# A matrix-state recurrence on one core: masked and turned chunk products interleaved under the state chain, and a query scaling without its own exponential

## What is computed

```python
def step(S, inp):
    r_t, d_t, k_t, v_t, kk_t, a_t = inp
    sk = jnp.einsum('bhvk,bhk->bhv', S, kk_t)
    S = (S * d_t[:, :, None, :] - sk[..., None] * (kk_t * a_t)[:, :, None, :]
         + v_t[..., None] * k_t[:, :, None, :])
    return S, jnp.einsum('bhvk,bhk->bhv', S, r_t)
```

## Time and profile before

| | us |
|---|---|
| median of 3 runs | 3968.01 (3967.4 to 3968.58) |
| the profiled execution, its own time | 3959.53 |
| its span in the profile | 3957.7 |
| PE busy in the span | 3685.2 (93%) |
| DVE busy | 2278.2 (58%) |
| ACT busy | 825.3 (21%) |
| mean granted clock of PE | 0.978 of full speed |

### The profile page before, as it was taken

The page is one execution under the profiler, slowest core; times in us unless marked ns, Lnnn a source line. Parts: engine busy times, 40 slices in busy tenths (PEclk is TensorE's granted clock), DMA queues, the critical chain, the costliest instruction groups (busy, mean ns, idle before and its releaser), DMA issues. The chain is left out here.

```text
span 3957.7 us, 73111 instructions
## 1 busy us (share of the span) xinstructions
PE 3685.2 (93%) x31536; PEld 2846.8 (72%) x31536; DVE 2278.2 (58%) x3422; ACT 825.3 (21%) x1844; POOL 741.0 (19%) x504
## 2 busy tenths in 40 slices
PE   7999788888899999999998999999967999999997
PEld 4888566666666888877776777777644788887886
DVE  8441677776446666672646455556555666666253
ACT  6110444333221110010112222222223101101000
POOL 1221000000022222213432101001002222221343
PEclk9999899999899999999999999999988999999999
DMA  2222111100121111112322111111482111112232
GB/s 81 84 75 85 61 32 37 34 30 27 65 88 45 36 45 45 45 61 82 114 78 72 49 43 51 40 47 40 138 310 109 47 45 45 45 35 80 82 110 75
DMA packets 119160, 268.30 MB, mean 68 GB/s; under 512 B 38073, under 2 KB 59961, under 8 KB 116409
## 3 DMA queue, kind: packets, MB, share of 16 engines
q1 hardware_dynamic: 118840, 263.63, 19.2%
HBM read 214.64 MB, written 48.95 MB: 67 GB/s over the span
## 5 line engine op out<-in xcount | busy, mean ns | idle before, releaser
L403 PE MATMUL ps<-sb_h,sb_w 128*128 128x272 f32 x1672 | 408.1, 392 | 1.4 <-ACT sb_tmp L563 1.4
L403 PEld LDWEIGHTS ps<-sb_h,sb_w 128*128 128x128 f32 x1672 | 317.5, 190 | 67.6 <-issue 2.3
L403 PE MATMUL ps<-sb_x,sb_w 128*128 128x272 f32 x1216 | 291.1, 392 | 0.0
L403 PEld LDWEIGHTS ps<-sb_x,sb_w 128*128 128x128 f32 x1216 | 231.0, 190 | 47.6
L460 PE MATMUL ps<-sb_big,sb_w 128*128 128x272 f32 x1056 | 251.6, 397 | 2.5 <-issue 1.3
L460 PEld LDWEIGHTS ps<-sb_big,sb_w 128*128 128x128 f32 x1056 | 202.5, 192 | 46.5 <-issue 4.3
L766 DVE SCALAR_TENSOR_TENSOR sb_big<-sb_tmp,sb_big 128x1024 f32<-128x1024 f32 (+1 forms) x176 | 203.4, 1156 | 13.2
L1454 PE MATMUL ps<-sb_x,sb_w 128*128 128x272 f32 x768 | 183.8, 392 | 0.0
L373 PE MATMUL ps<-sb_h,sb_w 128*128 128x384 f32 (+1 forms) x576 | 177.1, 469 | 3.9 <-DVE sb_tmp L741 2.1
L2682 PE MATMUL ps<-sb_h,sb_w 128*128 128x384 f32 (+1 forms) x528 | 171.8, 468 | 0.0
L1454 PEld LDWEIGHTS ps<-sb_x,sb_w 128*128 128x128 f32 x768 | 145.9, 190 | 30.1
(11 more groups left out here) (415 smaller groups left out, 7015.9 us busy)
## 6 DMA issues: line engine op xcount, KB each, us to landing
sb_w<-wup SPq DMA_DIRECT2D x88, 512.0 KB, 4.5
sb_w<-wdown SPq DMA_DIRECT2D x48, 704.0 KB, 4.2
sb_w<-wqkv SPq DMA_DIRECT2D x33, 512.0 KB, 3.7
sb_w<-wrkv SPq DMA_DIRECT2D x24, 512.0 KB, 5.6
sb_tmp<-wdown SPq DMA_DIRECT2D x16, 704.0 KB, 4.2
sb_x<-kT SPq DMA_DIRECT2D x10, 1024.0 KB, 12.1
rkv_scratch<-sb_big SPq DMA_DIRECT2D x18, 544.0 KB, 6.5
sb_big<-vc SPq DMA_DIRECT2D x9, 1024.0 KB, 11.7
```

The source lines that it names most:

```text
L403: mm = pe.matmul(m.ps[:, 2 * HOME[f][p] + e, 0:PIECE], w, rhs[:, k, e * PIECE:(e + 1) * PIECE], start=(k == 0 and p not in ("P2", "P3")), ...
```

## The change

`PIPE` and the three orders now alternate: two masked units, the two turned units that had come late, and one gate unit, three times (`at` `bt`, `kq` `kt`, `rb` `vt`), and then `rk` and `bv`. `CHAIN` follows that order. DVE does `normal_key`, the addition and the decay of the samples' state one each between the two steps that go with the turned units. In `decays` the subtraction is gone, in `powers` its exponential; `scale_q` multiplies Q by `EP` of the token before, in each chunk from its second token on (in the sample chunk in each group of 8), with a drain ahead of it.

```diff
--- before.py
+++ after.py
@@ -1475,11 +1475,13 @@
     SC = NCH - 1
     LAST = PAIRS - 1
 
+    FRONT = (("at", "bt"), ("kq", "kt"), ("rb", "vt"), ("rk", "bv"))
     PIPE = [(0, "sa", 0), (0, "sa", 1), (0, "sa", 2), (0, "kn")]
     for i in range(PAIRS):
         prev, ahead = i > 0, i < LAST
         gate = [[(i + 1, "sa", g)] if ahead else [] for g in range(3)]
-        PIPE += [(i, "at"), (i, "kq"), (i, "rb")] + gate[0] + [(i, "rk")] + ([] if i else [(0, "bonus")]) + gate[1] + [(i, "bt")] + gate[2] + [(i, "kt"), (i, "vt"), (i, "bv")]
+        for n, (masked_st, turned_st) in enumerate(FRONT):
+            PIPE += [(i, masked_st)] + ([(0, "bonus")] if n == 3 and not i else []) + [(i, turned_st)] + (gate[n] if n < 3 else [])
         PIPE += ([(i - 1, "ys")] if prev else []) + [(i, "t0")]
         for l in range(1, 6):
             PIPE += [(i, f"t{l}"), (i, f"z{l - 1}")]
@@ -1502,9 +1504,7 @@
         who = "a" if u[1] in BY_ACT else "d"
         counts[who] += 1
         TAKEN[u] = (who, counts[who])
-    CHAIN = {}
-    for n, st in enumerate(("at", "kq", "rb", "rk", "bt", "kt", "vt", "bv")):
-        CHAIN[st, 0], CHAIN[st, 1] = 2 * n + 1, 2 * n + 2
+    CHAIN = {u: n + 1 for n, u in enumerate((st, half) for st in ("at", "bt", "kq", "kt", "rb", "vt", "rk", "bv") for half in range(2))}
     STEPS = PC
     APART = {"at", "kq", "rb", "rk", "bv", "t1", "x1", "t2", "x2", "G", "H", "yl"}
     WHOLE = {"t0", "qt"}
@@ -1724,8 +1724,7 @@
 
             def powers(j):
                 act.wait_ge(prep_d, prepared(j, "diff"))
-                act.activation(EP, LS, ACT.Exp, scale=-DEC)
-                act.activation(SG, SG, ACT.Exp, scale=-DEC).then_inc(acts, 1)
+                act.activation(EP, LS, ACT.Exp, scale=-DEC).then_inc(acts, 1)
 
             def inverse_powers(j):
                 act.activation(LS, LS, ACT.Exp, scale=DEC)
@@ -1769,14 +1768,10 @@
             for i in range(PAIRS):
                 ahead = i + 1 if i < LAST else None
                 act.wait_ge(prep_d, prepared(i, "ready"))
-                if ahead:
-                    gates(ahead, 0)
-                    gates(ahead, 1)
-                turned_out(i, "bt", BTc)
-                if ahead:
-                    gates(ahead, 2)
-                turned_out(i, "kt", KTc)
-                turned_out(i, "vt", VTc)
+                for n, (st, dst) in enumerate((("bt", BTc), ("kt", KTc), ("vt", VTc))):
+                    turned_out(i, st, dst)
+                    if ahead:
+                        gates(ahead, n)
                 if ahead:
                     squares(ahead)
                 out(i, "bv", BVc)
@@ -1820,9 +1815,7 @@
 
             def decays(j):
                 wait_taken(dve, j, "sa", 2)
-                dve.tensor_tensor_scan(LS, reset, SG, 0.0, ALU.mult, ALU.add)
-                dve.drain()
-                dve.tensor_tensor(SG, LS, SG, ALU.subtract).then_inc(prep_d, 1)
+                dve.tensor_tensor_scan(LS, reset, SG, 0.0, ALU.mult, ALU.add).then_inc(prep_d, 1)
 
             def keys(j):
                 dve.tensor_scalar(EI, A, -1.0, col(j, PKA), ALU.add, ALU.mult)
@@ -1862,7 +1855,10 @@
 
             def scale_q(j):
                 dve.wait_ge(acts, ACTS[j, "powers"])
-                dve.tensor_tensor(Qt[j % 2], Qt[j % 2], SG, ALU.mult)
+                dve.drain()
+                for lo, hi, n in ((0, SEQ, C), (SEQ, T, NS)):
+                    q, before = (t[:, lo:hi].rearrange("p (c s) -> p c s", s=n) for t in (Qt[j % 2], EP))
+                    dve.tensor_tensor(q[:, :, 1:n], q[:, :, 1:n], before[:, :, 0:n - 1], ALU.mult)
 
             def scale_b(j):
                 dve.wait_ge(acts, ACTS[j, "inverses"])
@@ -1881,22 +1877,19 @@
                 dve.scalar_tensor_tensor(out=dst, in0=m.ps[:, 7, 0:HD], scalar=pend[i % 2][:, c:c + 1],
                                          in1=Nc[:, c, :], op0=ALU.mult, op1=ALU.add).then_inc(std, 1)
 
-            def steps(i, *sts):
...
-            def mask(i, st, which, dst):
-                for half in range(2):
-                    if i and CHAIN[st, half] < PC:
-                        step(i - 1, CHAIN[st, half])
-                    wait_full(dve, i, st, half)
-                    ins = dve.tensor_tensor(octet(dst, half), octet_ps(i, st, half), bc2(ms[:, which, :]), ALU.mult)
-                    for r, src in samples_out(i, st) if half else []:
-                        ins = dve.tensor_tensor(dst[r, SC, :], src, ms[r, which + 2, :], ALU.mult)
-                    ins.then_inc(outd, 1)
+            def chained(i, st, half):
+
+                if i and CHAIN[st, half] < PC:
+                    step(i - 1, CHAIN[st, half])
+
+            def mask(i, st, which, dst, half):
+
+                chained(i, st, half)
+                wait_full(dve, i, st, half)
+                ins = dve.tensor_tensor(octet(dst, half), octet_ps(i, st, half), bc2(ms[:, which, :]), ALU.mult)
+                for r, src in samples_out(i, st) if half else []:
+                    ins = dve.tensor_tensor(dst[r, SC, :], src, ms[r, which + 2, :], ALU.mult)
+                ins.then_inc(outd, 1)
 
             def add_states(i):
 
@@ -1912,11 +1905,13 @@
                     wait_full(dve, i, "mean", half)
                     dve.tensor_tensor(flat(YT, half), flat(YT, half), flat_ps(i, "mean", half), ALU.subtract).then_inc(outd, 1)
 
-            def sample_state(i):
+            def add_sample_state(i):
                 if i:
                     dve.wait_ge(out_s, 16 * i)
                 dve.wait_ge(small_ps, SUMS[i, "samples"])
                 dve.tensor_tensor(sout[:, 0:NB, :], m.ps[:, 6, :].rearrange("p (b v) -> p b v", b=NB), sbc, ALU.add)
+
+            def decay_sample_state(i):
                 dve.drain()
                 dve.tensor_tensor(sout[:, 0:NB, :], sout[:, 0:NB, :],
                                   pend[i % 2][:, PC:PC + NB].unsqueeze(2).broadcast_to([P, NB, HD]), ALU.mult).then_inc(sst, 1)
@@ -1983,17 +1978,30 @@
             scale_r(0).then_inc(prep_d, 1)
             for i in range(PAIRS):
                 ahead = i + 1 if i < LAST else None
-                mask(i, "at", 0, ATc)
-                mask(i, "kq", 0, KQc)
-                mask(i, "rb", 1, RBc)
-                mask(i, "rk", 1, RKc)
+                for half in range(2):
+                    mask(i, "at", 0, ATc, half)
+                chained(i, "bt", 0)
+                if ahead:
+                    normal_key(ahead)
+                chained(i, "bt", 1)
+                for half in range(2):
+                    mask(i, "kq", 0, KQc, half)
+                chained(i, "kt", 0)
+                if i:
+                    add_sample_state(i - 1)
+                chained(i, "kt", 1)
+                for half in range(2):
+                    mask(i, "rb", 1, RBc, half)
+                chained(i, "vt", 0)
+                if i:
+                    decay_sample_state(i - 1)
+                chained(i, "vt", 1)
+                for half in range(2):
+                    mask(i, "rk", 1, RKc, half)
                 if not i:
                     bonuses(0)
-                if ahead:
-                    normal_key(ahead)
-                if i:
-                    sample_state(i - 1)
-                steps(i - 1, "bt", "kt", "vt", "bv")
+                for half in range(2):
+                    chained(i, "bv", half)
                 if ahead:
                     decays(ahead)
                 if i:
@@ -2043,7 +2051,8 @@
                 if ahead:
                     scale_k(ahead)
                     bonuses(ahead)
-            sample_state(LAST)
+            add_sample_state(LAST)
+            decay_sample_state(LAST)
             for c in range(1, PC):
                 step(LAST, c)
             add_states(LAST)
@@ -2251,21 +2260,23 @@
                 Qch, Rch = ch(Qt[i % 2]), ch(Rt[i % 3])
                 pe.wait_ge(prep_d, prepared(i, "ready" if i else "keyed"))
                 chunks(i, "at", [(Bc, Qch)], "plain", "crossed")
+                turn(i, "bt", Bc)
+                if ahead:
+                    gates(ahead, 0)
                 chunks(i, "kq", [(Kc, Qch)], "plain", "crossed")
+                turn(i, "kt", Kc)
+                if ahead:
+                    gates(ahead, 1)
                 pe.wait_ge(prep_d, prepared(i, "ready"))
                 chunks(i, "rb", [(Bc, Rch)], "plain", "crossed")
+                if not i:
+                    pe.wait_ge(ld_v, 16)
+                turn(i, "vt", Vc)
                 if ahead:
-                    gates(ahead, 0)
+                    gates(ahead, 2)
                 chunks(i, "rk", [(Kc, Rch)], "plain", "crossed")
                 if not i:
                     bonus(0)
-                if ahead:
-                    gates(ahead, 1)
-                turn(i, "bt", Bc)
-                if ahead:
-                    gates(ahead, 2)
-                turn(i, "kt", Kc)
-                turn(i, "vt", Vc)
```

(16 more changed lines are left out.)

## The result

The changed kernel took 3939.31 us (median of 4 executions) against 3967.7 for the kernel before (median of 4): ratio 0.9931, 95% interval 0.9914 to 0.9948. It is faster, by 28 us where 15 were forecast, and lies under the range of 3946 to 3963. The profiled execution took 3936.94 us, 22.6 under the profiled one of before.

What follows compares the result with a forecast made beforehand. Fronts were taken as bound in turn by DVE, PE and DVE; -8.8 us at full clock and -6 from the clock gave -14.8, profiled 3959.5 to 3944.7, median 3968.0 to 3953; range 3946 to 3963.

Steps and rivals of the forecast that it cites:

- The subtraction: DVE's subtraction after the scan, on the path in fronts 1 to 6: removing it saves 1.21 us each, 7.3 in all.
- The held normal_key: DVE's normal_key beside POOL's product is held 1.26 us; gate unit covers 0.7, leaving 0.5 per front, 3.0 more in all.
- (1): Rival: the clock falls as before, leaving only -8.8 us: 3959.2 us; chance 0.2.
- (2): Rival: normal_key isn't held and no clock fall is left, -19.5 us: 3948.5 us; chance 0.13.
- (3): Rival: the subtraction's gain is lost because the inversion meets another wait: 3960.5 us; chance 0.1.
- (4): Rival: slower, fronts run at 1.2 GHz with transposes and waits mixed throughout: 3985 us; chance 0.06.
- front 0: Pair 0's front: normal_key's fetched keys come late and hold DVE, +0.5 us, bounds -1 and +2.8.
- The last front: Pair 7's front, with nothing ahead: 17.6 us instead of 19.6 at full clock, 2.0 less.
- the walk: PE, DVE and ACT queues of a front written side by side with unit costs, trusted to some tenths; it reproduced 22.5 us.
- the order at full clock: New unit order in fronts of pairs 1 to 6: DVE's scan starts 0.57 us earlier, 3.4 less in all.
- The clock: Lower clock costs 7.7 us in fronts, begun behind PE's 2.31 us gap; 6 taken as saved, with one fall left.
- scale_q: DVE's scaling of Q, split in two with a drain, ahead of E: +0.2 us per pair, 1.4 more in seven.

Runs made afterwards that it cites:

- e3: Kernel before, units' order and algebra untouched, with only DVE's normal_key and two sample-state halves set apart between steps of bt, kt, vt: 3942.66 us, ratio 0.9951.
- e9: Changed kernel with normal_key and both sample-state halves put together again ahead of step 11, restoring a long PE wait: 3964.5 us, ratio 1.000.
- e1: Changed kernel's new order with the old algebra (subtraction, its exponential, old scale_q): 3951.32 us, ratio 0.9965.
- e7: Kernel before's order of units, with DVE's three instructions set apart and the new algebra: 3932.67 us, ratio 0.9909.
- e2: Kernel before with the new algebra alone, old order of units: 3959.78 us, ratio 0.999.
- e6: Changed kernel with normal_key and the addition of the sample state exchanged, so normal_key is clear of POOL: 3939.83 us, ratio 0.9925.
- e10: Changed kernel measured again, unchanged, for a second trace: 3944.71 us, ratio 0.9954.
- e4: Kernel before measured again, unchanged, for a second trace: 3968.35 us, ratio 1.001.
- e5: Changed kernel with scale_q's small instruction (56 elements) put first: 3940.39 us, ratio 0.9932.
- e8: e7 with scale_q's small instruction put first: 3936.47 us, ratio 0.9921.
- e11: e7 with DVE taking E out of PSUM ahead of scale_q: 3935.03 us, ratio 0.9928.

## Why the prediction was wrong

**The mechanism was right, and so were most steps.** DVE's three instructions in a row and PE's long wait were the thing (e3, e9). The subtraction, said to be worth 1.21 us per front, gave 1.07 between e1 and the changed kernel (130.0 and 123.6 us in six fronts; 1.37 in the shortest, the rest went to PE's waits at `ys`), 1.02 between e3 and e7 (20.37 less 19.35) and 0.97 in e2. The held normal_key came true (1.83 us; the hold 1.04, I had 1.26), and so did most of its cover by the gate unit: 0.3 left per front by e6 for the 0.5 I took. POOL had begun 0.16 us earlier, and normal_key ended 0.59 us after it, not 0.79. The Trainium skill (SBUF — State Buffer, "Who interferes with whom") has the second one fully blocked until the first finishes; these rows agree with it, but for the first part of an instruction. scale_q's small one, 0.21 us when free, ended 0.08 after POOL's, and the 1.29 us of the earlier trace rows ended 1.14 after: in the three cases 0.13 to 0.20 us of the instruction's time passed during the hold, so that my 1.76 for 1.29 agreed less closely than I said (held for all of it, 1.91). The rivals fall: the clock does not fall as before in the fronts (1), normal_key is held (2), the subtraction's gain is there (3), and no front runs at 1.2 GHz (4). The preparation gave 1.4 for 1.0, and front 0 cost 0.3 for 0.5. The last front is 18.43 us long where the walk had 17.6; 0.47 of it is a wait at `ys`, and e10 has 17.73. No run takes the exponential out alone; the 1.0 us per front of e2 and e7 leaves nothing for it beside the subtraction's 1.21.

**The step that failed is the first term of the sum, the order at full clock.** I priced it at 0.57 us per front, less 0.5 for the hold: 0.4 us in six fronts. The kernel before has 135.3 us in its six fronts without the three falls, e1 130.0, hold included: 5.3 us. The walk had DVE's scan start 17.0 us after the first mask, and 17.5 with the hold. It starts at 16.77 or 16.78 in every front from 1 to 6 of e1 and of the changed kernel's three traces, and at 16.45 without the hold (e6), for 17.6 to 17.7 at full clock before. A group took PE 4.98 us in the walk, the third 4.88; the trace has 4.77 for the second (655.79 to 660.56) and 4.61 for the third. The first can't be set beside them, since its first unit runs ahead of the front's first mask. Of the 0.21 us that the second group is shorter, a product unit with its step has 0.07 (0.72 for 0.79), the gate unit 0.05 (0.70 for 0.75), and the step behind the long mask 0.11 (657.61 to 658.90, 1.29 for 1.40); the units with samples and the turned ones cost what I had to within 0.03. The two groups and the smaller rest of the hold make some 0.7 us per front. In the old order DVE sets the pace of the masked half, so that prices of PE that are too high don't show there, and the walk's agreement with 22.51 was a weak test of them; no run tries that by itself.

**The clock was taken too low.** I kept one fall and took 6 of 7.7 us; in the fronts 1 to 7 of all three traces of the changed kernel there is none. Falls between the fronts come in either kernel: two in the first trace of before and three in e4's, none, two and two between fronts 1 and 7 in the changed kernel's.

**scale_q was taken too low as well, and it didn't matter.** I had 1.4 us. PE's wait for E grew by 6.3, and scale_q takes 2.18 us per pair, over the 2 at which I said that it would take most of the order's gain; it didn't. I had a row with such a hold next to it and didn't ask which DVE instruction would now stand beside POOL's product. e5, e8 and e11 take most or all of that wait away and gain nothing that can be measured. All three traces have more of PE's waits without a releaser than the same kernel's without the edit (22.2 us for 17.6 to 20.4, 19.2 and 18.5 for 12.3 and 14.9), which is what PE meeting its next wait would look like; with one trace each it isn't shown.

**The range was cut by the baseline.** I moved the forecast by the difference between one profiled execution and the median, as if it were a constant. It was a single good execution (e4). 76 executions spread over 22 us, so with a profile of before from one end and four executions of the changed kernel from the other the range had to be wider by some 5 us on each side.

**The sum.** The two profiled executions differ by 22.6 us where I had 14.8, 7.8 more: 4.9 from the order, 1.7 from the clock, 0.6 from the preparation and front 0 and 2.2 from the rest of the program, less 0.9 for the subtraction and 0.8 for the last front. The stretches between fronts grew by the 1.4 us that I had, and that is luck: the other traces have 401.2 (before) and 404.5 and 401.0 (changed). The other 6 of the 14 us between 3953 and 3939.3 are the baseline. Against all executions together (3942.1 and 3965.9, 24 us) the error is 9, against the three comparisons (22 us) 7.

## What to carry to other kernels

Look for instructions that no one waits for, standing in a row ahead of one in a chain that another engine waits for: taking them apart, one to each link, gave more (22 us, e3) than the reordering of the units with the same taking apart in it (13 us, e1). When a walk of the queues gives the old time, that tests only the prices of the engine that sets the pace there; look for a stretch that tests those of the engine that will set it afterwards. Before two engines' work is shifted, list what each will stand beside afterwards: in this kernel POOL held DVE twice, once mostly covered by a gate unit, and once ahead of a wait whose removal gained nothing. And run a comparison more than once before its size is explained: the same two kernels gave 28, 18 and 19 us.

## What was not expected of the hardware

One long wait per front was enough for the clock to fall in all seven fronts of e9, 2.56 us in six and 1.74 in the last; in the kernel before it fell in three of six with 2.31 us and in the last with 2.05, while the wait of 1.42 us in the changed kernel's front of pair 1 brought no fall. The six middle fronts took 2.9 to 4.4 us more than the changed kernel's, of which the walk explains 2.3. That wait cost 20 us in all, against the changed kernel beside it (e10).

Outside the fronts shorter waits go with falls. Between fronts 1 and 7 the fifteen traces have 21, each 0.1 to 2.4 us behind a wait of PE of 0.9 to 1.5 us. 19 of them begin in one of two places, some 16.2 or 53 to 55 us after the front's end: behind a wait for DVE in the one, behind one without a releaser in the other. What sets these places apart from others with such waits was not tried.

PE also waits 12 to 22 us in the recurrence for nothing that the profile shows, in 16 to 34 pieces, and more in the later pairs: in the changed kernel's trace 0.8 us between 520 and 600 us and 3.9 between 920 and 1000. The stretch from one front to the next grows with it, from 55.9 us after front 1 to 58.8 after front 6, and in like manner in the other kernels. In the alternating orders some of them stand in the fronts, at `ys`; with the old order of units the fronts 1 to 7 have none. What makes them was not tried; it stays open. Of the scatter between executions the part that goes with the list of granted clocks is large: over the 25 executions of before beside e1, a straight line gives 2.8 us less for each 0.001 more of mean clock, and two thirds of the variance.
